# An encoder kernel in two layers: rows of maxima read back from memory, three PSUM banks passed on, later requests for the next layer's weights

## The chip, the core and the metric

The kernel runs on one core of a Trainium2 chip. The metric is the time of one execution on the device in microseconds (us). The kernel before takes 1848.21 us, the median of three runs from 1846.54 to 1849.18.

## What is computed

Two layers (DEPTH = 2) of an encoder over 256 tokens of width 2048, all in f32. Each layer normalises x, projects it, runs three mixers side by side, adds their joint projection to x, and adds a mixture of experts. Cut to what matters here:

```python
for l in range(DEPTH):
    xn = rms_norm(x, norm_mix[l])
    c_q, c_kv, k_rope, dq, dk, dv, mu, mv, mo, mg = jnp.split(xn @ w_in[l], split_at, axis=-1)
    y_mla = mla_mixer(...)          # 8 heads, dense attention
    y_dil = dilated_mixer(...)      # 12 heads, dilated attention with a bias
    y_ml = mlstm_mixer(...)         # 4 heads, forward and backward
    x = x + jnp.concatenate([y_mla, y_dil, y_ml], axis=-1) @ w_out[l]
    x = x + hier_moe(rms_norm(x, norm_ffn[l]), ...)   # 16 experts, 2 of them per token

# in mlstm_scan, for each head and direction, with m the running maximum of a token
a = jnp.exp(logw - m[..., None]) * jnp.einsum('bhtd,bhsd->bhts', qc, kc)
```

The weight matrix `a` of a head needs the negated maximum of every query token in every partition (key token): a row of 256 numbers per direction, spread over 128 partitions. These rows are what the change is about.

## The kernel before, in words

There is one instruction stream per engine, written out by hand in order and tied by semaphores: TensorE (PE) multiplies, VectorE (DVE) and ScalarE (ACT) copy results out of PSUM and do the arithmetic between, SyncE (SP) asks for the weights, GpSimd (POOL) asks for a few other transfers.

**Order of a layer on TensorE.** (1) The projections c0, c1, c2 (L1012 to L1033), then mu0, lat, mu1, up, mu2 (L1038 to L1065) and the gate rows. (2) Seven pairs of projection blocks, `product(name, u)` for u = 0 to 6 with seven products p1, p6, c11, w, p5, c21, c12 each, and one single block m14. The steps of the two attentions run between these products. (3) `queries_keys(0)`, `row_of_maxima(0)` and `(1)` (L1135 to L1137), then the output projection A, `product_a(name, u)` for u = 0 to 3. The rest of the mLSTM mixer runs between its products: scores, values, `queries_keys(1)`, `row_of_maxima(2)` and `(3)` (L1140 to L1162). (4) The output projection B. (5) The router and the experts in eight pairs i = 0 to 7, with blocks g0, u0, g1, u1 and the down projections dy0 to dy3. (6) At the end of the layer a branch over code for overfull experts (L1344 to L1385, not taken here) and the last scatter, sc0 to sc7 (L1387 to L1390), which adds the last pair's result to x.

**Rows of maxima.** `gate_rows` on VectorE (L1694 to L1712) leaves the negated maxima in `neg_m`, four partitions (the heads) by two directions by 256 tokens. `row_of_maxima(h)` (L911 to L917) spreads head h to all 128 partitions with two matmuls of a selecting column, into PSUM bank `w{h}`. From there VectorE adds gates and mask on the diagonal blocks (`masked`, L1787 to L1795), and ScalarE takes exponentials (`decays`, L2366 to L2374). VectorE multiplies with the scores (`weighted`, L1797), and TensorE reads the result in `values` (L935).

**PSUM banks.** Eight banks are given out by a table made ahead of time, `plan_banks` (L200 to L283) and `plan_queries_keys` (L316 to L324). `freed(name)` waits until the previous user of the name's bank has been copied out; `copied(name)` waits for the name itself. Before the change `bias`, mu0, mu2 and the first product p1 of stage 2 all use bank 0. The queries and keys mqa, mqb, mqc use banks 2, 3 and 4, and w0 to w3 use banks 6, 7, 5 and 5. The last dilated output do5 stands in bank 3, and `queries_keys` waits for all three of its banks before its first matmul (L891).

**Weights.** SyncE works through one list of requests in order. Each waits until its slot of a ring of six (with three spare places outside the ring) has been read for the last time (`load`, L671 to L675). In the next layer the list goes c0, c1, c2, `up`, mu0, mu1, mu2, mw, m0 and so on (L681 to L700).

**GpSimd's requests.** Per layer: in the second layer x is stored (L785) and the bias table is read again (L790). Then, in both layers, it waits for the last product of stage 2 (`c12_6`, L791) and reads x back (L794), because X holds sums during stage 2. VectorE waits for x before it adds the first product of A (L1962).

Of the kernel before, what the change touches and what calls it, by code (L numbers as in the profile page):

```python
# [20 lines left out]
F32 = mybir.dt.float32  # L21
# [5 lines left out]
P = 128  # L27
# [172 lines left out]
def plan_banks():  # L200

    b = Uses(8)
    b.once("bias", 0)
# [11 lines left out]
    b.once("mu2", 0)  # L215
# [15 lines left out]
    for u in range(N_APAIR):  # L231
        for name in PRODUCTS:
# [4 lines left out]
            if at in MLSTM_AT:  # L237
# [9 lines left out]
                if h == 2:  # L247
                    b.once("w3", 5)
# [67 lines left out]
def plan_queries_keys(b, g):  # L316

    for n, c in enumerate("abc"):
        b.once(f"mq{c}{g}", 2 + n)
    if g == 0:  # L320
        b.once("w0", 6)
        b.once("w1", 7)
    else:
        b.once("w2", 5)  # L324
# [76 lines left out]
def build(nc, a, consts, onehot, lncount, out):  # L401
    with ExitStack() as ctx:
# [42 lines left out]
        x_dram = nc.dram_tensor("x_dram", (P, KT, S), F32).ap()  # L445
        bias_dram = nc.dram_tensor("bias_dram", (H_D, 2 * S), F32).ap()
# [40 lines left out]
        vf = v_mla[:, :, :].rearrange("p t n -> p (t n)")  # L487
        hs = scr[:, 0:8 * CAP].rearrange("p (k n) -> p k n", k=4)
# [68 lines left out]
        for name, n in (("sq", 4), ("sq_sum", 1), ("xg_even", KT // 2), ("xg_odd", KT // 2), ("rstd_x", 1), ("xn_n", 1), ("a_sums", 1), ("w_sums", 3 * N_PAIR), ("lat_std", 1), ("lat_n", 1),  # L557
# [3 lines left out]
                        ("masked", H_M), ("r_ready", H_M), ("m_std", 1), ("o_gate", 1), ("y_ml", 1), ("w_rg", 1), ("sq2", N_OUT), ("acc2", N_OUT),  # L561
# [104 lines left out]
        def _(sp):  # L666
# [14 lines left out]
            for l in range(DEPTH):  # L681
# [10 lines left out]

                load("up", l, a["w_up"][l], width=3 * W_D + 1024)
# [70 lines left out]
        def _(pool):  # L764
# [16 lines left out]
            for l in range(DEPTH):  # L781
                if l:
# [7 lines left out]
                    pool.dma_start(BIAS[:, :, :], bass.AP(bias_dram.tensor, 0, [[1, P], [2 * S, H_D], [1, S + P]])).then_inc(bias_out, 16)  # L790
                pool.wait_ge(*ready(f"c12_{N_PAIR - 1}", l))  # L791
                if l:
                    pool.wait_ge(x_out, 16 * l)
                pool.dma_start(X[:, :, :], x_dram if l else a["x_t"]).then_inc(x_back, 16)  # L794
            pool.wait_ge(x_back, 16 * DEPTH)
# [3 lines left out]
        def _(pe):  # L799
# [86 lines left out]
            def queries_keys(g, l):  # L886
# [4 lines left out]
                for i in "abc":  # L891
                    pe.wait_ge(*freed(f"mq{i}{g}", l))
# [3 lines left out]
                for n in range(2):  # L896
# [4 lines left out]
                    last_b = mm(o[2], w_qk[low, n, b, H_TOP:HD_M], uc[low, b, :], False, True)  # L901
                    mm(o[1][top, :], w_qk[:, n, a, P:HD_M], uc[:, a, :], True, False)
# [7 lines left out]

            def row_of_maxima(h, l):  # L911

                name = f"w{h}"
                pe.wait_ge(*freed(name, l))
                for d in range(2):
                    last = mm(bank(name)[:, d * S:(d + 1) * S], K[0:H_M, h:h + 1].to_broadcast([H_M, P]), grow(d, 0))
                last.then_inc(*made(name))  # L917
# [94 lines left out]
            for l in range(DEPTH):  # L1012
# [123 lines left out]
                for h in range(2):  # L1136
                    row_of_maxima(h, l)  # L1137
# [1398 lines left out]
```

## Time and profile before

| | |
|---|---|
| Median of 3 runs | 1848.21 us (1846.54 to 1849.18) |
| The profiled execution, its own time | 1849.53 us |
| Its span, first to last instruction | 1847.6 us |
| TensorE busy | 1825.8 us, 99% of the span |
| VectorE, ScalarE, GpSimd busy | 738.0, 313.4, 8.5 us |
| Moved by DMA | 544.78 MB, mean 295 GB/s |
| Mean granted TensorE clock | 0.997 of full speed |

The profiled execution is one execution of its own: its time is 1.3 us above the median of the runs. Times inside a profile count from the start of the span. A busy TensorE is not one at its peak, since matmuls are pipelined and their ends are modelled. Each f32 matmul stands in the trace as two records of MATMUL and two of LDWEIGHTS.

### The profile page before, as it was taken

To read this page: it belongs to the slowest core of one execution; us is meant where nothing else is said; L and a number is where in the kernel's file an instruction comes from. 1 tells how busy PE (TensorE), PEld (TensorE's weight loads), DVE (VectorE), ACT (ScalarE), POOL (GpSimd) and SP (SyncE) were. 2 spreads that over 40 slices of the span, in tenths; PEclk is the share of its full clock that TensorE was granted. 3 is DMA by queue.
4 is the path that set the end of the run, shared out by engine and by line. 5 is a ranking of instruction groups with operands and counts; after the bars stand their busy time and mean duration, and the time that the engine had idled before them with its cause. 6 is when DMAs were issued, how large, how long until landed. Compare 5 with 4: busy or idle time off the path is not lost.

```text
span 1847.6 us, 28284 instructions
## 1 busy us (share of the span) xinstructions
PE 1825.8 (99%) x12270; PEld 1384.1 (75%) x12270; DVE 738.0 (40%) x1531; ACT 313.4 (17%) x846; POOL 8.5 (0%) x17
## 2 busy tenths in 40 slices
PE   9999999999999999999899999999999999999998
PEld 8788887899765667666597888878996666666655
DVE  3467665576202122021235675655661022121123
ACT  3123122211201111011021131231121111111010
POOL 1000000000000000000000000000000000000000
PEclk9999999999999999999999999999999999999999
DMA  9433343437999999999964342352479999999995
GB/s 384 157 139 140 134 166 156 158 146 276 361 423 422 427 427 428 426 427 427 408 238 155 125 183 103 154 204 110 193 274 368 423 424 428 427 427 427 427 427 245
DMA packets 46702, 544.78 MB, mean 295 GB/s; under 512 B 5240, under 2 KB 5368, under 8 KB 12912
## 3 DMA queue, kind: packets, MB, share of 16 engines
q1 hardware_dynamic: 44784, 531.47, 70.1%
q0 software_dynamic: 1792, 11.46, 1.6%
q8 instruction: 101, 1.65, 0.4%
q14 instruction: 25, 0.20, 0.0%
HBM read 538.68 MB, written 4.22 MB: 294 GB/s over the span
## 4 chain that ended last, share of the span: by engine, by line
PE 96%; DVE 2%; DMA 1%; issue 1%; ACT 0%; SPq 0%; DVEq 0%
PE ps L801 93%; PE ps L855 1%; DMA ring<-in_w_main 1%; PE ps L1270 1%; PE ps L871 0%; PE ps L1169 0%; DMA ring<-in_w_lat 0%; PE ps L863 0%; DVE ring L1660 0%; PE ps L1324 0%; DVE ss_a L1686 0%; DVE ss_a L1685 0%; DVE XN L1950 0%; DVE ring L1900 0%; DVE ring L1845 0%
## 5 line engine op out<-in xcount | busy, mean ns | idle before, releaser
L801 PE MATMUL ps<-ring,scr 128*64 128x256 f32 (+2 forms) x3488 | 626.6, 424 | 4.1 <-issue 4.1
L801 PEld LDWEIGHTS ps<-ring,scr 128*64 128x64 f32 (+1 forms) x3488 | 337.5, 138 | 216.0 <-issue 123.9
L801 PE MATMUL ps<-ring,XN 128*128 128x256 f32 (+2 forms) x1184 | 242.4, 361 | 2.9 <-DMA ring<-in_w_lat 1.7
L801 PEld LDWEIGHTS ps<-ring,XN 128*128 128x128 f32 x1184 | 210.7, 190 | 23.9 <-issue 4.5
L801 PE MATMUL ps<-ring,X 128*128 128x256 f32 x896 | 200.6, 379 | 0.0
L801 PE MATMUL ps<-XN,ring 128*128 128x128 f32 (+1 forms) x1312 | 196.0, 306 | 1.9 <-DVE X L1933 0.9
L801 PEld LDWEIGHTS ps<-XN,ring 128*128 128x128 f32 x1312 | 180.2, 191 | 15.0 <-issue 4.1
L801 PEld LDWEIGHTS ps<-ring,X 128*128 128x128 f32 x896 | 169.6, 190 | 22.7
L801 PE MATMUL ps<-PR,scr 128*64 128x256 f32 (+2 forms) x704 | 173.8, 402 | 0.0
L2119 DVE TENSOR_TENSOR v_mla<-scr,ps 128x256 f32<-128x256 f32 x32 | 13.5, 422 | 390.5 <-PE ps L801 390.5
L801 PE MATMUL ps<-BIAS,scr 128*64 128x256 f32 (+1 forms) x608 | 157.2, 414 | 0.0
L801 PE MATMUL ps<-XN,scr 128*64 128x256 f32 (+1 forms) x480 | 143.1, 455 | 0.0
L801 PE MATMUL ps<-PR,prob 128*128 128x256 f32 x512 | 119.1, 386 | 4.8 <-issue 4.8
L801 PE MATMUL ps<-v_mla,PR 128*128 128x128 f32 x1024 | 119.2, 276 | 1.0 <-DVE v_mla L2075 1.0
L801 PEld LDWEIGHTS ps<-v_mla,PR 128*128 128x128 f32 x1024 | 116.2, 192 | 5.1 <-issue 5.1
L801 PEld LDWEIGHTS ps<-PR,scr 128*64 128x64 f32 (+1 forms) x704 | 98.0, 144 | 25.6 <-issue 3.4
L801 PEld LDWEIGHTS ps<-PR,prob 128*128 128x128 f32 x512 | 95.9, 192 | 24.0 <-issue 11.9
L2143 DVE COPY prob<-ps 128x512 f32<-128x512 f32 x32 | 22.1, 692 | 207.4 <-PE ps L801 207.4
L801 PEld LDWEIGHTS ps<-BIAS,scr 128*64 128x64 f32 x608 | 81.8, 137 | 29.6 <-issue 2.9
L2446 ACT ACTIVATE scr<-ps,par 128x128 f32<-128x128 f32 x240 | 64.7, 407 | 219.2 <-PE ps L801 219.2
L2083 DVE TENSOR_TENSOR X<-X,ps 128x512 f32<-128x512 f32 x128 | 88.0, 688 | 31.5 <-PE ps L801 30.6
L801 PEld LDWEIGHTS ps<-XN,scr 128*64 128x64 f32 x480 | 65.8, 138 | 34.2 <-issue 25.0
(276 smaller groups left out, 1457.7 us busy)
## 6 DMA issues: line engine op xcount, KB each, us to landing
ring<-in_moe_w_gate SPq DMA_DIRECT2D x42, 2048.0 KB, 20.3
ring<-in_moe_w_down SPq DMA_DIRECT2D x38, 2048.0 KB, 23.0
ring<-in_w_main SPq DMA_DIRECT2D x36, 2048.0 KB, 9.3
ring<-in_moe_w_up SPq DMA_DIRECT2D x36, 2048.0 KB, 19.3
ring<-in_w_out_a SPq DMA_DIRECT2D x16, 1280.0 KB, 5.9
PR<-in_moe_w_up SPq DMA_DIRECT2D x10, 2048.0 KB, 16.1
XN<-in_moe_w_down SPq DMA_DIRECT2D x10, 2048.0 KB, 19.6
BIAS<-in_moe_w_up SPq DMA_DIRECT2D x10, 2048.0 KB, 18.7
```

Source lines behind the costliest of these rows:

```text
L801: return pe.matmul(o, lhsT, rhs, start=start, stop=stop, skip_group_check=True)
L855: last = pe.transpose(bank(name)[:, (kt * NT + t) * P:(kt * NT + t + 1) * P], prob[:, u % 2, j, t, kt * P:(kt + 1) * P], ident)
L1270: last = pe.transpose(bank(name)[:, q * 2 * CAP:(q + 1) * 2 * CAP], gated[:, (2 * half + q) * P:(2 * half + q + 1) * P], ident)
L2083: dve.tensor_tensor(x, x, bank(name), ALU.add).then_inc(*read(name))
L2119: dve.tensor_tensor(gated[:, half * CH:(half + 1) * CH], sgs[:, half * CH:(half + 1) * CH], bank(f"u{half}_{i}")[0:2 * CAP, 0:CH], ALU.mul ...
L2143: dve.tensor_copy(Y[:, n * 512:(n + 1) * 512], bank(f"dy{n}_{i}")[0:2 * CAP, :]).then_inc(*read(f"dy{n}_{i}"))
L2446: ins = act.activation(XG[:, 4 * n + k, :], bank(name)[:, k * 2 * CAP:(k + 1) * 2 * CAP], ACT.Copy, scale=pcol(l, R_FFN + 4 * n + k))
```

## The change

Four parts. Rows of maxima: GpSimd stores `neg_m` to memory once per layer (4 KB), and reads each head's two rows back with a partition step of zero, so that they land in all 128 partitions (256 KB per head). They land in the place of `v_mla`, two heads at a time. `row_of_maxima` goes, and `masked` and `decays` read SBUF. Heads 0 and 1 are asked for after the last output of the first attention (`ao3`), heads 2 and 3 after x has been asked for and the place's last user is done (`decayed`, a signal that takes the part of the freed bank). Banks: `bias` goes to bank 1, mu2 to bank 2. For the queries and keys mqc and mqb swap places in the first group, and the bank of mqc is waited for only after four matmuls. Requests: in the second layer SyncE waits for the previous layer's sc0 of the last scatter before it asks for `up` and all that follows it in its list.

```diff
--- before.py
+++ after.py
@@ -200,7 +200,7 @@
 def plan_banks():
 
     b = Uses(8)
-    b.once("bias", 0)
+    b.once("bias", 1)
     b.part = "layer"
     for j in range(3):
         b.once(f"c{j}", 4 + j)
@@ -212,7 +212,7 @@
     for t in range(NT):
         for j in range(4):
             b.once(f"up{t}{j}", [4, 5, 6, 7, 2, 3, 4, 5][4 * t + j])
-    b.once("mu2", 0)
+    b.once("mu2", 2)
     for d in range(2):
         b.once(f"rows{d}", 6 + d)
     for u in range(N_PAIR):
@@ -244,8 +244,6 @@
                         b.once(f"ms{h + j2}", ((5, 4), (2, 3))[h // 2][j2])
                 if h == 1:
                     plan_queries_keys(b, 1)
-                if h == 2:
-                    b.once("w3", 5)
             if at == MIX_AT:
                 for y in range(5, KT // 2):
                     b.once(f"y{y}", y - 3)
@@ -315,13 +313,8 @@
 
 def plan_queries_keys(b, g):
 
-    for n, c in enumerate("abc"):
-        b.once(f"mq{c}{g}", 2 + n)
-    if g == 0:
-        b.once("w0", 6)
-        b.once("w1", 7)
-    else:
-        b.once("w2", 5)
+    for c, n in zip("abc", (2, 4, 3) if g == 0 else (2, 3, 4)):
+        b.once(f"mq{c}{g}", n)
 
 
 
@@ -443,6 +436,8 @@
         sweep_load, sweep_pe, sweep_act, sweep_dve, sweep_own = map(
             sem, ("sweep_load", "sweep_pe", "sweep_act", "sweep_dve", "sweep_own"))
         x_dram = nc.dram_tensor("x_dram", (P, KT, S), F32).ap()
+        maxima_dram = nc.dram_tensor("maxima_dram", (H_M, 2 * S), F32).ap()
+        maxima_out, maxima_in = sem("maxima_out"), [sem(f"maxima_in{b}") for b in range(2)]
         bias_dram = nc.dram_tensor("bias_dram", (H_D, 2 * S), F32).ap()
 
         ident, flip = K[:, K_ID:K_ID + P], K[:, K_FLIP:K_FLIP + P]
@@ -485,6 +480,7 @@
         combT = scr[0:NE, 1536:1536 + S]
 
         vf = v_mla[:, :, :].rearrange("p t n -> p (t n)")
+        maxima = vf[:, 0:4 * S].rearrange("p (b d s) -> p b d s", b=2, d=2)
         hs = scr[:, 0:8 * CAP].rearrange("p (k n) -> p k n", k=4)
         sgs = scr[0:2 * CAP, 512:512 + F_E]
         XG = scr[:, 1024:1024 + KT * 2 * CAP].rearrange("p (k n) -> p k n", k=KT)
@@ -558,7 +554,7 @@
                         ("a_roped", 1), ("a_sq", 1), ("a_ss", 1), ("a_std", 1), ("a_n", 1),
                         ("d_sq", 2), ("d_ss", 2), ("u_conv", 1), ("v_ones", 1), ("rb", 1), ("d_std", 1), ("d_n", 1), ("nmax", H_A), ("d_exp", H_D), ("p_scaled", H_A + H_D),
                         ("gate_b", 1), ("gate_ln", 2), ("rows_ready", 2), ("em_ready", 1), ("uc_ready", 1),
-                        ("masked", H_M), ("r_ready", H_M), ("m_std", 1), ("o_gate", 1), ("y_ml", 1), ("w_rg", 1), ("sq2", N_OUT), ("acc2", N_OUT),
+                        ("masked", H_M), ("decayed", H_M), ("r_ready", H_M), ("m_std", 1), ("o_gate", 1), ("y_ml", 1), ("w_rg", 1), ("sq2", N_OUT), ("acc2", N_OUT),
                         ("ya_sums", 2), ("a1", N_APAIR), ("a2", N_APAIR), ("a3", N_APAIR), ("a4", N_APAIR),
                         ("y_sums", 2), ("t1", N_BPAIR), ("t2", N_BPAIR), ("t4", N_BPAIR),
                         ("e_in", 2), ("e_exp", 2), ("picked", 1), ("flags", 1), ("gm", NE), ("gw", NE // 2),
@@ -690,6 +686,8 @@
                 for j in (1, 2):
                     load(f"c{j}", l, a["w_lat12"][l, j - 1], width=KT * LAT[j][1])
 
+                if l:
+                    sp.wait_ge(*ready(f"sc0_{NE // 2 - 1}", l - 1))
                 load("up", l, a["w_up"][l], width=3 * W_D + 1024)
                 for j in range(W_M // CH):
                     load(f"mu{j}", l, a["w_main"][l, 3 * W_D // CH + j])
@@ -788,10 +786,27 @@
                     pool.wait_ge(*ready(LAST_READER[last], l - 1))
                     pool.wait_ge(*ready("mu0", l))
                     pool.dma_start(BIAS[:, :, :], bass.AP(bias_dram.tensor, 0, [[1, P], [2 * S, H_D], [1, S + P]])).then_inc(bias_out, 16)
+                def load_maxima(h):
+
+                    pool.dma_start(maxima[:, h % 2, :, :].rearrange("p d s -> p (d s)"),
+                                   bass.AP(maxima_dram.tensor, h * 2 * S, [[0, P], [1, 2 * S]])).then_inc(maxima_in[h % 2], 16)
+
+                pool.wait_ge(*after("rows_ready", l, 1))
+                if l:
+                    pool.wait_ge(maxima_in[0], 16 * H_M // 2 * l)
+                    pool.wait_ge(maxima_in[1], 16 * H_M // 2 * l)
+                pool.dma_start(maxima_dram, neg_m[:, :, :].rearrange("h d s -> h (d s)")).then_inc(maxima_out, 16)
+                pool.wait_ge(maxima_out, 16 * (l + 1))
+                pool.wait_ge(*ready(f"ao{H_A // 2 - 1}", l))
+                load_maxima(0)
+                load_maxima(1)
                 pool.wait_ge(*ready(f"c12_{N_PAIR - 1}", l))
                 if l:
                     pool.wait_ge(x_out, 16 * l)
                 pool.dma_start(X[:, :, :], x_dram if l else a["x_t"]).then_inc(x_back, 16)
+                for h in range(2, H_M):
+                    pool.wait_ge(*after("decayed", l, h - 2))
+                    load_maxima(h)
             pool.wait_ge(x_back, 16 * DEPTH)
             pool.wait_ge(bias_out, 32 + 16 * (DEPTH - 1))
 
@@ -888,7 +903,7 @@
                 a, b, c = 3 * g, 3 * g + 1, 3 * g + 2
                 top, low = slice(0, H_TOP), slice(H_TOP, P)
                 out = [[bank(f"mq{i}{g}")[:, n * S:(n + 1) * S] for i in "acb"] for n in range(2)]
-                for i in "abc":
+                for i in "ab":
                     pe.wait_ge(*freed(f"mq{i}{g}", l))
                 if g == 0:
                     pe.wait_ge(*after("uc_ready", l))
@@ -899,6 +914,8 @@
                     mm(o[2], w_qk[:, n, c, H_TOP:HD_M], uc[:, c, :], True, False)
                     last_a = mm(o[0], w_qk[top, n, b, 0:P], uc[top, b, :], False, True)
                     last_b = mm(o[2], w_qk[low, n, b, H_TOP:HD_M], uc[low, b, :], False, True)
+                    if n == 0:
+                        pe.wait_ge(*freed(f"mqc{g}", l))
                     mm(o[1][top, :], w_qk[:, n, a, P:HD_M], uc[:, a, :], True, False)
                     mm(o[1][low, :], w_qk[:, n, c, 0:H_TOP], uc[:, c, :], True, False)
                     if n == 1:
@@ -907,14 +924,6 @@
                     mm(o[1][top, :], w_qk[top, n, b, P:HD_M], uc[top, b, :], False, True)
                     last = mm(o[1][low, :], w_qk[low, n, b, 0:H_TOP], uc[low, b, :], False, True)
                 last.then_inc(*made(f"mqc{g}"))
-
-            def row_of_maxima(h, l):
-
-                name = f"w{h}"
-                pe.wait_ge(*freed(name, l))
-                for d in range(2):
-                    last = mm(bank(name)[:, d * S:(d + 1) * S], K[0:H_M, h:h + 1].to_broadcast([H_M, P]), grow(d, 0))
-                last.then_inc(*made(name))
 
             def scores(g, l):
 
@@ -1133,8 +1142,6 @@
                         step(NT * j + t - 1)
 
                 queries_keys(0, l)
-                for h in range(2):
-                    row_of_maxima(h, l)
                 pe.wait_ge(*copied(f"ao{H_A // 2 - 1}", l))
                 pe.wait_ge(*copied(f"do{H_D // 2 - 1}", l))
                 for u in range(N_APAIR):
@@ -1156,8 +1163,6 @@
                                 scores(h // 2, l)
                             if h == 1:
                                 queries_keys(1, l)
-                            if h in (1, 2):
-                                row_of_maxima(h + 1, l)
                         if at == MIX_AT:
                             mixed(l)
                 for q in range(5, KT // 2):
@@ -1787,16 +1792,16 @@
                 def masked(h):
                     if h == 0:
                         dve.wait_ge(*copied("gcols", l))
-                    dve.wait_ge(*ready(f"w{h}", l))
+                    dve.wait_ge(maxima_in[h % 2], 16 * (H_M // 2 * l + h // 2 + 1))
                     for d in range(2):
                         for at, t, b in DIAGONAL[d]:
-                            ins = dve.scalar_tensor_tensor(decay[:, h % 2, d, at:at + P], bank(f"w{h}")[:, d * S + t * P:d * S + (t + 1) * P],
+                            ins = dve.scalar_tensor_tensor(decay[:, h % 2, d, at:at + P], maxima[:, h % 2, d, t * P:(t + 1) * P],
                                                            gcol[:, 0, d, b, h:h + 1], masks[d], ALU.add, ALU.add)
                     ins.then_inc(*signal("masked"))
 
                 def weighted(h):
                     dve.wait_ge(*ready(f"ms{h}", l))
-                    dve.wait_ge(*copied(f"w{h}", l))
+                    dve.wait_ge(*after("decayed", l, h))
                     for d, lo, hi, src in ((0, 0, S, 0), (0, S, S + P, S + P), (1, 0, P, 0), (1, P, P + S, S)):
                         w = decay[:, h % 2, d, lo:hi]
                         ins = dve.tensor_tensor(w, w, bank(f"ms{h}")[:, src:src + hi - lo], ALU.mult)
@@ -2367,11 +2372,11 @@
                     act.wait_ge(*after("masked", l, h))
                     for d in range(2):
                         at, t, b = ACROSS[d]
-                        act.activation(decay[:, h % 2, d, at:at + P], bank(f"w{h}")[:, d * S + t * P:d * S + (t + 1) * P], ACT.Exp,
+                        act.activation(decay[:, h % 2, d, at:at + P], maxima[:, h % 2, d, t * P:(t + 1) * P], ACT.Exp,
                                        bias=gcol[:, 0, d, b, h:h + 1])
                         ends = decay[:, h % 2, d, :].rearrange("p (b n) -> p b n", n=P)[:, ::2, :]
                         ins = act.activation(ends, ends, ACT.Exp)
-                    ins.then_inc(*read(f"w{h}"))
+                    ins.then_inc(*signal("decayed"))
 
                 def one_way(g):
                     act.wait_ge(*after("r_ready", l, g))
```

## Rows read from the trace of the kernel before

**Rows 1.** Page, part 1: busy us (share of the span) and instructions of TensorE

```profile
PE 1825.8 (99%) x12270; PEld 1384.1 (75%) x12270; DVE 738.0 (40%) x1531; ACT 313.4 (17%) x846; POOL 8.5 (0%) x17
```

**Rows 2.** Waits of TensorE: total us, times, longest us

```profile
PE ps L801 <- issue: 10.0, 7, 3.8
...
PE ps L801 <- ACT PR L2287: 1.3, 2, 0.7
...
PE ps L801 <- DVE prob L1472: 0.9, 1, 0.9
```

**Rows 3.** Timeline, first layer, stage 3: start us, us, engine, line, records [idle before]

```profile
320.64 5.75 PE L801 MATMUL ps<-ring 128*128 128x256 f32 x32 [0.53 <-issue]
326.33 1.99 PE L801 MATMUL ps<-neg_m,K 4*128 4x256 f32 x8
328.25 2.50 PE L801 MATMUL ps<-PR,ring 128*128 128x128 f32 x20
...
354.94 1.12 PE L801 MATMUL ps<-neg_m,K 4*128 4x256 f32 x4
355.99 2.50 PE L801 MATMUL ps<-PR,ring 128*128 128x128 f32 x20
```

**Rows 4.** Tile neg_m: records on TensorE, ns min/median/max, first and last start

```profile
L801 PE MATMUL ps<-neg_m,K x32: 374/374/478, 326.3 to 1289.7; 4*128 4x256 f32 x32
```

**Rows 5.** Timeline of VectorE and TensorE, second layer, the same place

```profile
1246.42 2.15 DVE L1793 SCALAR_TENSOR_TENSOR scr<-ps,gcol,K 128x128 f32<-128x128 f32 x8
1249.54 0.69 DVE L1930 TENSOR_TENSOR X<-X,ps 128x512 f32<-128x512 f32 x1 [0.97 <-PE ps L801]
1250.14 0.42 DVE L1933 TENSOR_TENSOR X<-X,ps 128x256 f32<-128x256 f32 x1
...
1251.50 2.40 PE L801 MATMUL ps<-PR,ring 128*128 128x128 f32 x20
```

**Rows 6.** Request of x on GpSimd, landing times, and head 2's first use on VectorE

```profile
300.73 0.55 POOL L794 DMA_DIRECT2D X<-in_x_t  x1 [252.52 <-PE ps L801]
...
X<-in_x_t POOLq DMA_DIRECT2D x1, 2048.0 KB, 12.4
...
356.10 1.13 DVE L1793 SCALAR_TENSOR_TENSOR scr<-ps,gcol,K 128x128 f32<-128x128 f32 x4 [1.33 <-PE ps L801]
```

**Rows 7.** Windows: busy of PE, PEld, DVE, ACT, POOL (records); clock, DMA share, GB/s

```profile
450.00:460.00 10.00, 9.81 (x93) 8.58 (x92) 5.35 (x11) 3.39 (x7) 0.00 (x0) 1.00 0.44 156
...
860.00:870.00 10.00, 10.00 (x78) 5.41 (x76) 0.69 (x1) 0.60 (x1) 0.00 (x0) 1.00 1.02 433
```

**Rows 8.** Timeline of TensorE, where block g1 of expert pair 7 starts, each layer

```profile
879.29 0.40 PE L801 MATMUL ps<-ring,scr 128*64 128x256 f32 x1 [1.45 <-issue]
...
1797.94 0.46 PE L801 MATMUL ps<-ring,scr 128*64 128x256 f32 x1 [2.41 <-issue]
```

**Rows 9.** Timeline around the last scatter, each layer, and the first read of mu0

```profile
908.45 0.33 SPq L675 DMA_DIRECT2D ring<-in_w_lat  x1
...
915.80 0.33 SPq L675 DMA_DIRECT2D ring<-in_w_up  x1
...
919.53 8.83 PE L801 MATMUL ps<-PR,prob 128*128 128x256 f32 x32 [3.76 <-issue]
...
959.42 13.98 PE L801 MATMUL ps<-XN,ring 128*128 128x256 f32 x64
...
1836.65 7.14 PE L801 MATMUL ps<-PR,prob 128*128 128x256 f32 x32 [1.05 <-issue]
```

**Rows 10.** Windows of 2 us at the two last scatters, columns as in rows 7

```profile
922.00:924.00 2.00, 2.00 (x6) 1.55 (x6) 1.34 (x3) 0.51 (x1) 0.00 (x0) 0.50 1.14 475
...
1834.00:1836.00 2.00, 1.61 (x8) 0.29 (x4) 0.34 (x1) 0.00 (x0) 0.00 (x0) 1.00 0.00 0
```

**Rows 11.** DMA: last w_lat request to landing; the instruction queue from 916.8 to 918

```profile
ring<-in_w_lat SPq DMA_DIRECT2D x1, 1472.0 KB, 12.6
...
q8 instruction: 1, 0.02, 5.6%
```

## The prediction

> **What bounds the kernel.** I read the page first: TensorE is busy for 1825.8 us of 1847.6, and no other engine is near that [rows 1]. So a microsecond taken from TensorE's stream counts in full, unless a transfer then sets the pace. I read the waits of TensorE next, which sum to little: 10.0 us without a releaser, the longest 3.8, then 1.3 and 0.9 us for two copies out of PSUM [rows 2]. Third came the timelines of the places that the change touches, and last the DMA share in windows, because the experts' weights come at close to the engines' full rate: a share of 0.44 shortly before the experts, but 1.02 near their end [rows 7].
>
> **Rows of maxima: what goes.** Each layer loses eight matmuls, 32 records in both layers [rows 4]. What counts is the distance from their first start to the next product's start, not the records' own 374 ns, since they overlap. For heads 0 and 1 that is 328.25 - 326.33 = 1.92 us, and for one later head 355.99 - 354.94 = 1.05 us [rows 3]; the other later head repeats the latter. Per layer 1.92 + 2 x 1.05 = 4.02 us, twice: **8.0 us**. All of it is on TensorE's own chain. The switch from narrow tiles to full ones stays, as the work in front of the rows has narrow tiles too.
>
> **Rows of maxima: what comes.** Per layer one store of 4 KB and four reads of 256 KB, on GpSimd's queue. In the first layer x is asked for at 300.73 and lands 12.4 us later; head 2 is first used on VectorE at 356.10 [rows 6]. Heads 0 and 1 are asked for even before x. Head 2 is asked for when head 0's exponentials are done, which is shortly after VectorE's `masked` work, whose counterpart in the second layer ends at 1246.42 + 2.15 [rows 5], so about 25 us before its use. No read of 256 KB had to be priced before; x, of 2 MB, took 12.4 us on this queue, so I take 0 and keep 12.4 us as the upper bound of one read, which still fits. If the cover went, `masked(2)` would wait on VectorE, with the evictions of A behind it and TensorE behind these. The DMA time of 1 MB per layer falls where the engines have room. That VectorE and ScalarE read SBUF in place of PSUM is off the chain.
>
> **What is late next.** `masked(0)` and `(1)` no longer wait for TensorE, but VectorE works in order, and TensorE now reaches A sooner. In the second layer `masked` ends at 1248.57, then VectorE needs 0.69 + 0.42 us for the first product p1, whose bank c11 takes over. c11 started at 1251.50 [rows 5] and wants to start 1.92 + 0.53 earlier, at 1249.05; p1's copy is ready at about 1249.6. So 0.5 us comes back, and I take **0.4 us lost**. In the first layer I reckon none.
>
> **Banks.** With `bias` in bank 1, mu0 needn't wait: 0.9 us once. With mu2 in bank 2, the first product needn't wait for mu2's copy: 1.3 us over both layers [rows 2]. With mqc late, `queries_keys(0)` starts before do5 is copied, and the four matmuls ahead of the wait cover the rest: 0.53 us [rows 3], twice. Sum **3.3 us**. The bounds are zero and this sum; I take the whole, since each is a gap in front of an idle engine with its inputs there.
>
> **Later requests.** In the first layer the last scatter starts after 3.76 us of idle time, in the second after 1.05, with the same code in front (a branch that isn't taken into the expert loop). Its records then take 8.83 us against 7.14 [rows 9], because the granted clock is 0.50, the 1.2 GHz level, right after the idle stretch [rows 10]. So the first layer pays 2.71 + 1.69 = 4.4 us more. What differs is the traffic: in the second layer the DMA share ahead of the scatter is 0.00 [rows 10]; in the first SyncE has asked for w_lat at 908.45 and `up` at 915.80 [rows 9]. TensorE jumps over the expert loop there, and a packet of the instruction queue is in flight between 916.8 and 918 [rows 11], before the scatter's start at 919.53.
>
> The Trainium skill (Runtime: NRT & Kernel Launch, Instruction fetch mechanics) says that a taken branch to a far target forces a fetch of the target's code by DMA before execution goes on. The two layers agree with that, and by this rule alone the whole 4.4 us would go with the traffic.
>
> But only part of the traffic is moved. The w_lat request at 908.45 takes 12.6 us to land [rows 11], to about 921, and stays where it is; the code packet starts only about 1 us after `up` is asked for. The bounds are 0 and 4.4 us; neither row is nearer, and **I take 2.0 us**. The cost of the delay itself is nothing: `up` goes out at the scatter's first result, some 2 us later, and mu0, behind it, is first read at 959.42 [rows 9].
>
> **Sum.** 8.0 + 3.3 - 0.4 + 2.0 = **12.9 us**. The profiled execution's own time, 1849.53 us, becomes 1836.6. It stands 1.3 us above the median of the runs; from the median, 1848.2, I predict **1835.3 us**. A measurement of this kernel can tell about 0.2%, 3.7 us, from no change.
>
> **Rivals.** Each keeps the 10.9 us of rows and banks where nothing else is said.
>
> *The code comes at once.* The scatter of the first layer starts as in the second: 4.4 us in place of 2.0, so 1832.9. For it speaks that the second layer has no more idle time than 1.05 us. Chance 0.27.
>
> *The code stands behind w_lat.* The late requests change nothing at the branch, and the time is 1837.3. For it speaks w_lat's landing at 921, after the scatter's start. The Trainium skill (DMA: Bandwidth & Descriptors, Queues, rings and completion order) has a DMA engine drain a whole packet of one queue before it serves another; by this the code may wait for w_lat's packet, and asking for `up` later would not help. Rows 11 fit, but don't prove it. Chance 0.25.
>
> *The weights eat the gain.* TensorE waits 1.45 and 2.41 us for blocks of the last expert pair [rows 8]: the stream of weights is the bound there. If its start were not tied to TensorE, all that TensorE saves before would come back as a longer wait: nothing left of the 10.9, so 1846.2, and 1848 if the longer idle time costs clock as well. Against it: the share of 0.44 at 450 to 460 us [rows 7] shows the stream still waiting for TensorE to release slots, after all that is removed. So it starts sooner by as much. Chance 0.06.
>
> *Rows come late: slower.* Heads 2 and 3 stand behind x on GpSimd's queue. If a read took longer than the 25 us that it has, by L us, each layer would lose about L; both layers together lose the 12.9 us gained from L = 6.5 us on, and it is a measurable loss from L = 8.3, that is a read of over 33 us. With 40 us: 1835.3 + 2 x 15 = 1865. Against it: x took 12.4 us with eight times the bytes. Chance 0.02.
>
> *The change doesn't do what it says*: rows still on TensorE, or banks that wait for another user. The bank table gives each of the moved names a bank that is long free, so 0.02, at about 1845.
>
> **Numbers.** The forecast has 0.38 and is the likeliest; the rivals have 0.27, 0.25, 0.06, 0.02 and 0.02. The low end is the code at once, no loss on VectorE and no half clock in the second layer's g1 either (1.7 us, priced like the scatter's): 1848.2 - 11.3 - 4.4 - 1.7 = 1830.8, so 1831.0. The high end is the code behind w_lat with one more stretch of half clock, 1837.3 + 1.7 = 1839.0, and half a microsecond of scatter: 1839.5. Faster by over 0.2% (under 1844.5): the first three, 0.90, and 0.03 from the others, 0.93. Within 0.2%: the weights' case, 0.05. Slower: 0.02.
>
> **What the new profile would show.** No records on neg_m from TensorE, and A's first product right behind `queries_keys`. No wait for L2287 or L1472, and no 0.53 us ahead of `queries_keys(0)`. In the second layer a short wait for VectorE at c11 of pair 0. The idle time ahead of the first layer's last scatter between 1.05 and 3.76 us, and whether the clock falls behind it, decides between the first three cases. The waits in front of g1 of pair 7 stay near 1.45 and 2.41; if they grow by several microseconds, the weights eat the gain. I am wrong if VectorE waits for a maxima transfer with TensorE behind it, or if a new gap opens where a bank changed its user.

## The result, and the profile after

The changed kernel took **1840.41 us** (median of 7 runs; the one at 1889.13 is disturbed and left out of the comparison, as is one of late_from_c2 below at 6933.86), the kernel before 1848.21. The ratio is 0.9947, 95% interval [0.9937, 0.9957]: 9.8 us less, between 7.9 and 11.6. The forecast was 1835.3, so 12.9 us less, with a range from 1831.0 to 1839.5. By the ratio the time is 1838.4, inside it; the median of the seven runs is 0.9 us above its high end, that of the six undisturbed ones, 1839.7, is 0.2 us above. A second set of runs of the same kernel (below) gave 1840.63 and 0.9946.

Page of the changed kernel: span, then part 1.

```profile
span 1837.3 us, 28234 instructions
PE 1818.3 (99%) x12238; PEld 1381.0 (75%) x12238; DVE 736.8 (40%) x1531; ACT 314.3 (17%) x846; POOL 13.9 (1%) x27
```

TensorE has lost 32 records and 7.5 us of busy time against [rows 1]: the rows of maxima. It remains the engine that bounds the kernel. The waits of TensorE, as in [rows 2]:

```profile
PE ps L816 <- issue: 9.5, 6, 4.9
PE ps L816 <- DMA ring<-in_w_lat: 2.0, 1, 2.0
PE ps L816 <- DVE eps L1452: 1.1, 1, 1.1
```

The two waits for copies, 1.3 and 0.9 us, are gone. But the longest wait has grown from 3.8 to 4.9 us. The timeline around stage 3 in the second layer, which answers to [rows 3, 5]:

```profile
1234.52 5.78 PE L816 MATMUL ps<-ring 128*128 128x256 f32 x32
...
1240.23 2.50 PE L816 MATMUL ps<-PR,ring 128*128 128x128 f32 x20
...
1240.95 2.18 DVE L1798 SCALAR_TENSOR_TENSOR scr<-v_mla,gcol,K 128x128 f32<-128x128 f32 x8
...
1243.05 0.68 DVE L1935 TENSOR_TENSOR X<-X,ps 128x512 f32<-128x512 f32 x1
1243.65 0.41 DVE L1938 TENSOR_TENSOR X<-X,ps 128x256 f32<-128x256 f32 x1
...
1244.80 1.39 PE L816 MATMUL ps<-PR,ring 128*128 128x128 f32 x11
```

`queries_keys(0)` has no 0.53 us in front of it, the first product follows it at once, and c11 of pair 0 starts without a wait. Last, the places where TensorE is idle, as in [rows 8, 9]; the third row is the last scatter of the first layer:

```profile
7.33 22.29 PE L816 MATMUL ps<-ring,XN 128*128 128x192 f32 x128 [1.98 <-DMA ring<-in_w_lat]
...
874.92 0.40 PE L816 MATMUL ps<-ring,scr 128*64 128x256 f32 x1 [1.89 <-issue]
...
916.31 8.75 PE L816 MATMUL ps<-PR,prob 128*128 128x256 f32 x32 [4.90 <-issue]
...
1789.42 0.40 PE L816 MATMUL ps<-ring,scr 128*64 128x256 f32 x1 [1.70 <-issue]
```

The stall that the late requests were to shorten is longer than before, 4.90 us against 3.76, and its records still take 8.75 us. SyncE's requests, the windows in the stall (columns as in [rows 7]), and the DMA queues between 911 and 916.3 us (packets, MB, share of the 16 engines):

```profile
892.97 11.44 SPq L671 DMA_DIRECT2D ring<-in_w_lat  x2
918.39 0.33 SPq L671 DMA_DIRECT2D ring<-in_w_up  x1
```

```profile
908.00:910.00 2.00, 2.00 (x12) 0.77 (x10) 0.00 (x0) 0.60 (x1) 0.00 (x0) 1.00 0.92 389
910.00:912.00 2.00, 1.41 (x8) 0.27 (x4) 0.55 (x1) 0.00 (x0) 0.00 (x0) 1.00 0.55 226
...
914.00:916.00 2.00, 0.00 (x0) 0.00 (x0) 0.00 (x0) 0.00 (x0) 0.00 (x0) 1.00 0.07 22
```

```profile
q1 hardware_dynamic: 53, 0.52, 23.8%
q8 instruction: 2, 0.03, 4.0%
```

So `up` did go out late, at 918.39. The only weights in the engines at the jump were those of w_lat, and TensorE stood idle all the same. The stall can be taken apart with the packets of the instruction queue, which carry TensorE's code. In the kernel before, the last product ends at 915.77, the code packet starts 1.09 us later, takes 1.07, and the scatter starts 1.60 after it: 3.76 us. In the changed kernel the product ends at 911.41, the packet starts 1.04 us later, takes 2.20, and 1.66 us follow: 4.90 (another code packet, at 911.94, is done before it). The growth is the time of the packet itself. In the second layer of the changed kernel the packet starts at 1823.87, 1.96 us *before* the product's end, and 0.53 us of idle time is left.

### The profile page after: what moved, and what is told of

The parts are those of the page before. It is cut to its first block, busy times and chain, and to the rows that moved or that the text cites. A ratio compares the mean times of both kernels' runs of the same rounds, so it can differ in the third digit from the quotient of the medians.

```text
span 1837.3 us, 28234 instructions
## 1 busy us (share of the span) xinstructions
PE 1818.3 (99%) x12238; PEld 1381.0 (75%) x12238; DVE 736.8 (40%) x1531; ACT 314.3 (17%) x846; POOL 13.9 (1%) x27
## 4 chain that ended last, share of the span: by engine, by line
PE 98%; DVE 1%; issue 1%; DMA 0%; SPq 0%; DVEq 0%
PE ps L816 94%; PE ps L870 1%; PE ps L1174 1%; PE ps L1275 1%; PE ps L886 0%; DMA ring<-in_w_lat 0%; PE ps L878 0%; PE ps L1329 0%; DVE XN L1955 0%; DVE ring L1905 0%; DVE ring L1850 0%; DVE ring L1840 0%; PE ps L1082 0%; PE ps L1055 0%; DVE X L1938 0%
```

## The experiments

What was open: is the code that the jump needs held up behind `up` (theory U), behind w_lat (theory L), or does the place of the code in its 16 KB packets decide (theory P)? And are rows and banks worth what they were priced at? Each run was compared with the kernel before in its own job; its medians there were 1848.84, 1848.27 and 1848.91.

### The late requests alone, four ways

**no_late** is the changed kernel without the wait:

```
-                if l:
-                    sp.wait_ge(*ready(f"sc0_{NE // 2 - 1}", l - 1))
                 load("up", l, a["w_up"][l], width=3 * W_D + 1024)
```

> The changed kernel without the late requests: `up` and what follows are asked for as soon as their slots are free, as before. If the late requests are worth something at the branch (theory U: the code packet stands behind `up`), the idle time ahead of the first layer's last scatter grows from the 4.90 us of the changed kernel to 7 us or more, and the time by 2 to 4 us. If the packet stands behind w_lat alone (theory L), the idle time stays between 3.5 and 5 us, its records stay at 8.8 us, and the time is that of the changed kernel, about 1838 to 1839, within 1 us.

Measured: 1839.21 us, ratio 0.9952 [0.9939, 0.9965], so the same as with the wait. Timeline of TensorE in no_late at the last scatter, then the queues from 914 to 916 us:

```profile
911.50 3.26 PE L814 MATMUL ps<-PR,prob 128*128 128x256 f32 x14 [3.45 <-issue]
916.96 4.15 PE L814 MATMUL ps<-PR,prob 128*128 128x256 f32 x18 [2.21 <-issue]
```

```profile
q1 hardware_dynamic: 65, 0.85, 102.5%
q8 instruction: 1, 0.02, 3.0%
```

There are two stalls. The one at the jump is there with and without `up` in the engines: over all profiles that ask for w_lat as before it is 2.94, 3.59 and 4.90 us with the late request, and 1.87, 2.80, 3.34, 3.45 and 3.76 without it (no_branch, which has no jump, left out). A second, of 2.21 us, opens in the middle of the scatter, while a code packet is in flight among the packets of `up`. The kernel before does not have it, and with the wait it is absent again: that is what the late request buys, for a stall that the other parts of the change had opened. The medians don't show it: 0.9952 against 0.9947 is within their intervals. What they leave open, the packets answer. The next code packet starts 3.18 us after the scatter in no_late, and 3.3 to 3.7 us after it in the four other profiles with w_lat and `up` asked for as before; with the late request it starts 0.6 us after it in all three.

**late_from_c1** moves the wait up, ahead of the loop that asks for c1 and c2 of w_lat; **late_from_c2** puts it ahead of c2 only.

```
+                if l:
+                    sp.wait_ge(*ready(f"sc0_{NE // 2 - 1}", l - 1))
                 for j in (1, 2):
                     load(f"c{j}", l, a["w_lat12"][l, j - 1], width=KT * LAT[j][1])
...
-                if l:
-                    sp.wait_ge(*ready(f"sc0_{NE // 2 - 1}", l - 1))
                 load("up", l, a["w_up"][l], width=3 * W_D + 1024)
```

> The changed kernel with the wait for sc0 two requests earlier, ahead of the w_lat loads c1 and c2. Theory L (the code packet stands behind the packets of w_lat): the idle time ahead of the first layer's last scatter falls from 4.90 us to the second layer's 0.5 to 1.1, the scatter's records fall from 8.75 to 7.15 us since the clock isn't lowered, and the time falls by 3.8 + 1.6 = 5.4 us or a little less, to about 1833. TensorE doesn't wait for c1, which has some 17 us from the request to its use. Theory U: no change at the branch. Theory P (the place of the code in its pages sets the stall, not traffic): no change at the branch either.

> The changed kernel with the wait for sc0 ahead of c2 alone; c1 is asked for as before. Theory L: the engines still have c0's and c1's packets when the code is asked for, but half of w_lat's bytes are gone, so the idle time is between 1 and 3.5 us, and the time between that of the changed kernel and that of the wait ahead of c1. Theories U and P: idle time stays at 4.9 us.

Measured: 1833.96 us, ratio 0.9927 [0.9914, 0.9941], and 1833.72 us, 0.9919 [0.9904, 0.9933]. The last scatter of the first layer in late_from_c1, and in late_from_c2:

```profile
910.06 7.17 PE L816 MATMUL ps<-PR,prob 128*128 128x256 f32 x32 [0.77 <-issue]
```

```profile
911.53 7.17 PE L816 MATMUL ps<-PR,prob 128*128 128x256 f32 x32 [1.46 <-issue]
```

With c1 and c2 out of the way the stall falls from 4.90 to 0.77 us, with only c2 out to 1.46, and the records take 7.17 us, the full clock. The DMA share of late_from_c1 is 0.03 from 905 to 909 us, where the changed kernel has 1.04, and its code packet starts 1.73 us before the last product ends, as in the second layer. Theory L holds for the stall at the jump. The cost of asking later is none that shows: the requests stand at 911.19, c1 and c2 land 7.6 us later in the median of the two, at about 917.3 and 920.8, and c0's products keep TensorE at work from 917.06 to 937.

**no_branch** leaves out on TensorE the branch and the loop for experts with more tokens than their slots hold, which this data never enters, and keeps w_lat as it is.

> The changed kernel without TensorE's code for overfull experts (the branch, the two register loads and the jumped-over loop are left out on TensorE; the inputs here never take it). All theories that put the stall on the jump (L, U and P) expect no idle time to speak of ahead of both last scatters, under 0.5 us, no lowered clock behind them, and 4.9 + 1.6 + 0.5 = 7.0 us less than the changed kernel, about 1831.5. If the idle time stays, the stall is not the jump's but that of a copy out of PSUM or of another wait.

Measured: 1830.51 us, ratio 0.9901 [0.9886, 0.9915]. Both last scatters start without idle time; the first layer's:

```profile
911.25 7.17 PE L816 MATMUL ps<-PR,prob 128*128 128x256 f32 x32
```

No code packet is in flight near this place (the next one starts at 920.07). So it takes both, a jump and w_lat's requests in flight. Either alone, late_from_c1 and no_branch show, costs less than 1 us. The run doesn't separate the jump from the two register loads and the wait for the flags that belong to the same code and went with it; for the jump speaks the code packet, which ends 1.5 to 1.7 us ahead of the scatter wherever the branch is kept.

### Each part on the kernel before

**only_rows** has the rows of maxima through memory and nothing else of the change; **only_banks** the bank numbers and the late wait for mqc; **only_late** the wait ahead of `up`; **before_late_c1** the wait ahead of c1, as above, but in the kernel before.

> The kernel before with the rows of maxima through memory alone: banks and the request for up stay as before. My sum: TensorE loses 4.02 us per layer, 8.0 us in all, the reads are hidden, and nothing or 0.4 us comes back at c11 of the second layer: ratio about 0.9957 (8.0 of 1848). The gaps of the banks must all still be there (0.9 and 0.68 us for the copies, 0.53 ahead of queries_keys(0)). If the rows were worth less than their distances on TensorE, because a transfer or VectorE takes over, the saving is well under 8 us and TensorE shows a wait for VectorE or for a maxima read. A shift of the last scatter against the pages of its code can add a second gap of about 2 us inside it, as in no_late, or not.

Measured: 1844.22 us, ratio 0.9977 [0.9968, 0.9985], 4.3 us less in place of 8.0. Timeline of TensorE in only_rows, both layers from `queries_keys(0)` to a later row of stage 3, and between them the end of the first layer:

```profile
320.46 5.75 PE L814 MATMUL ps<-ring 128*128 128x256 f32 x32 [0.53 <-issue]
...
460.12 5.44 PE L814 MATMUL ps<-v_mla,PR 128*128 128x128 f32 x32 [0.50 <-DVE v_mla L2076]
...
906.61 7.09 PE L814 MATMUL ps<-ring,scr 128*64 128x512 f32 x32 [1.74 <-issue]
916.50 4.95 PE L814 MATMUL ps<-PR,prob 128*128 128x256 f32 x14 [2.80 <-issue]
922.34 4.15 PE L814 MATMUL ps<-PR,prob 128*128 128x256 f32 x18 [0.89 <-issue]
...
1237.18 5.75 PE L814 MATMUL ps<-ring 128*128 128x256 f32 x32 [0.53 <-issue]
...
1377.07 3.81 PE L814 MATMUL ps<-v_mla,PR 128*128 128x128 f32 x32 [0.50 <-DVE v_mla L2076]
```

The same distance in only_late, which has the rows on TensorE, is 467.57 - 323.88 = 143.69 us in the first layer and 1387.61 - 1243.92 = 143.69 in the second. Here it is 139.66 and 139.89: **4.03 and 3.80 us** less, 7.8 in all. The six profiles with rows and banks changed in which no half clock falls into the distance have 139.67 to 139.70 in both layers. So the saving is there, and it is lost elsewhere. At the end of the first layer the idle times sum to 1.74 + 2.80 + 0.89 = 5.43 us against 3.76 before, in the second 0.75 + 0.95 = 1.70 against 1.05: 2.3 us back. The rest is clock: over its 12 runs the granted clock averaged 0.9961, over the 35 of the kernel before 0.9971, and 0.0010 of 1848 is 1.8 us. 7.8 - 2.3 - 1.8 = 3.7, beside 4.3 measured.

> The kernel before with bias in bank 1, mu2 in bank 2 and mqc late (its bank order too), all else as before. My sum: 0.9 + 1.3 + 2 x 0.53 = 3.3 us, ratio about 0.9982, and the three kinds of gap are gone from TensorE's waits while no new one opens. Rival: each gap moves to the next user of a bank or the next transfer, and the ratio is 1.000.

Measured: 1847.06 us, ratio 0.9986 [0.9974, 0.9998], 2.6 us less. The waits for L2287, for L1472 and the 0.53 us are gone, and no new one stands in their place. The last scatter of the first layer reads

```profile
920.15 7.14 PE L801 MATMUL ps<-PR,prob 128*128 128x256 f32 x32 [3.34 <-issue]
```

The stall at the jump was 3.34 us here, 0.4 less than before, and the mean clock 0.9965, worth 1.1 us: 3.3 + 0.4 - 1.1 = 2.6.

> The kernel before with only the wait ahead of the request for up. Theory L (the jump's code stands behind w_lat): the idle time ahead of the first layer's last scatter stays between 3 and 5 us, lowered clock behind it, and the time is that of before within 1 us, ratio 0.9995 to 1.0005. Theory U (it stands behind up): idle 1.1 us, no lowered clock, 4.4 us less, ratio 0.9976. Theory P (the place of the code in its pages decides whether a second fetch falls into the scatter): before had no second gap, so the wait has nothing to take away here and the time stays.

Measured: 1850.96 us, ratio 1.0015 [1.0006, 1.0024]: **slower**. Timeline of TensorE in only_late:

```profile
914.36 7.09 PE L803 MATMUL ps<-ring,scr 128*64 128x512 f32 x32 [1.87 <-issue]
924.39 8.83 PE L803 MATMUL ps<-PR,prob 128*128 128x256 f32 x32 [2.94 <-issue]
```

The stall at the jump stays, with the clock lowered behind it. There is no second stall for the wait to remove. Of the 2.8 us lost, 4.81 - 3.76 = 1.0 is the longer idle time at this place and 1.1 the mean clock (0.9965); 0.7 us stays open, within the interval. That the wait causes these is not shown; it gains nothing.

> The kernel before with the wait for the last scatter's first result ahead of the requests for c1, c2 and what follows, so that only c0 of w_lat is in flight at the jump. Theory L: the idle time ahead of the first layer's last scatter falls from 3.76 to about 1 us, the clock stays at full rate behind it, and the time is 4.4 us shorter, ratio 0.9976. Theory P (the place of the code): 3.76 us stay, ratio 1.000. If later requests have a price of their own, it shows as a wait of TensorE for c1 or c2 in the second layer, up to 2 us.

Measured: 1845.74 us, ratio 0.9987 [0.9978, 0.9996], 2.4 us less, in place of 4.4. The mechanism is as expected, since the last scatter of the first layer reads

```profile
915.24 7.14 PE L803 MATMUL ps<-PR,prob 128*128 128x256 f32 x32 [1.02 <-issue]
```

with 3.76 - 1.02 = 2.74 us less idle time and the full clock. The 1.7 us of lowered clock that should have gone too don't show in the median: the mean clock of its 12 runs, 0.9975, is only 0.0004, 0.7 us, above that of the kernel before. 2.74 + 0.7 = 3.4 us, and the interval reaches from 0.7 to 4.1.

### The same kernels again, and the code shifted

> The kernel after, unchanged, to see what of its profile is fixed and to compare it with the next run on the same chip. If the place of its stall is fixed by the program, the idle time ahead of the first layer's last scatter is 4.9 us again; if the 4.90 was one draw of when the code packets meet the packets of w_lat, it lies anywhere from 3 to 5. The median should come at about 1840, ratio 0.9947.

Measured: 1840.63 us, ratio 0.9946 [0.993, 0.9961]. In its profile the stall ahead of the last scatter is 3.59 us, and the last product of the experts has one of its own:

```profile
906.16 7.09 PE L816 MATMUL ps<-ring,scr 128*64 128x512 f32 x32 [1.52 <-issue]
916.83 8.83 PE L816 MATMUL ps<-PR,prob 128*128 128x256 f32 x32 [3.59 <-issue]
```

So the same program shows 4.90 and 3.59 us, and the growth from 3.76 is no fixed effect of the change.

> The kernel late_from_c1 again, in one job with the kernel after. Theory L: under 1 us of idle time ahead of the first layer's last scatter again, and the time is that of the kernel after less 3 to 5 us, ratio to before about 0.9925. Rival (its time was luck with stretches of lowered clock): the medians of the two differ by under 1.5 us.

Measured: 1831.89 us, ratio 0.9903 [0.9887, 0.992], 8.7 us under the changed kernel in the same job, more than the 3 to 5 expected. The last scatter of the first layer:

```profile
910.40 7.44 PE L816 MATMUL ps<-PR,prob 128*128 128x256 f32 x32 [0.79 <-issue]
```

The spans of the two profiles differ by 1839.0 - 1829.4 = 9.6 us: 3.59 - 0.79 = 2.8 is the stall, 1.7 the clock behind it, 1.5 - 0.2 = 1.3 the wait ahead of the last product, and 3.4 are two more stretches of half clock in after_again, where this profile has none before its very end; 0.4 is left. That the edit removes those two is not shown; the stall and the clock behind it, 4.5 us, are what it accounts for. With ratios of 0.9927 and 0.9903 in two jobs this kernel beats both the kernel before and the changed one, and keeps all the code.

**no_late_shifted** is no_late with three wide warm-up products less and thirteen narrow ones more at the start:

```
-            keep_running(0, 10)
+            keep_running(0, 7)
+            for _ in range(13):
+                mm(ps[:, 0, 0:1], ones[:, :], ones[:, 0:1])
```

> The kernel no_late with 40 instructions more on TensorE at the program's start (three wide warm-up products less, thirteen of one column more), hidden in its wait for the first weights, so that all of TensorE's code lies 40 instructions later against the borders of its 16 KB packets. If the 2.21 us of idle time inside the first layer's last scatter are the code packet behind the packet border that lay after 14 of its records, that gap must go, the one ahead of the scatter (w_lat) stays at 3 to 5 us, and the time is about 2 us less than that of no_late (ratio 0.994). Rival: if the gap were a wait for PSUM or for a copy, it stays at the same record whatever the place of the code. Another border may come to lie where it costs: in the last scatter of the second layer at most 0.6 us, as its engines are idle.

Measured: 1838.10 us, ratio 0.9935 [0.992, 0.9949], against 0.9952 for no_late, in line with 2 us, though the intervals overlap. The last scatter of the first layer is whole again:

```profile
916.66 7.14 PE L814 MATMUL ps<-PR,prob 128*128 128x256 f32 x32 [1.87 <-issue]
```

The stall in its middle is gone by moving code alone. The engine's inputs were the same, and the DMA engines as full (share 1.00 from 918 to 920 us, against 1.05 from 914 to 916 in no_late). So it was a code packet. In no_late and only_rows, both without the rows and without the wait, the border lay after the same 14 records; in the kernel before there is no stall in the scatter, so the border must lie elsewhere. That is the part of theory P that holds. The stall at the jump, 1.87 us, was shorter than the 3 to 5 us that I expected.

## Why the prediction was right, and where it failed

**Rows of maxima, 8.0 us: right.** The distances give 4.03 + 3.80 = 7.8 us in only_rows, and 4.0 us in each layer with the banks changed too. The reads cost nothing: four a layer, 3.5 us each from request to landing (x, the row I bounded them with, took 12.2). Head 2's was requested at 329.24 and VectorE first used it at 352.00.

**What comes back, 0.4 us: it didn't.** I let c11 wait for p1's copy, behind `masked`. But `masked` needs no records of TensorE any more, and it began 0.72 us after p1 began (1240.95 against 1240.23). The copy of p1 was done at 1244.06, and c11 started at 1244.80. From the start of `queries_keys(0)` to c11 it is 10.28 us, where it was 12.17 with the same two products between: 1.89 us less, all of what the row of maxima had cost. The reckoning had put the end of `masked` where it was before, at 1248.57, while TensorE alone moved.

**Banks, 3.3 us: right**, by the rows in only_banks and in the changed kernel; none of the gaps moved to another user of a bank.

**Later requests, 2.0 us: wrong.** This is the step that failed. I had put the stall down to traffic in general and, between 0 and 4.4 us, taken about the middle, though the last code packet started only about 1 us after `up` was asked for. At the jump the late request took nothing off: the stall comes with w_lat's requests, all of which were out before `up` was asked for, and it goes when they are held back (0.77, 0.79 and 1.02 us). The rival "The code stands behind w_lat", with 1837.3 us and a chance of 0.25, was the right one. The sum with 0 for this term and for the loss at c11 is 8.0 + 3.3 = 11.3 us, beside 9.8 measured (7.9 to 11.6). That the time still fell into the range is no merit of the 2.0 us: the range had its high end from this rival, and it lies 3.1 us from the forecast and 1.1 us from the rival's figure. The Trainium skill (DMA: Bandwidth & Descriptors, Queues, rings and completion order) has an engine drain a whole packet of one queue before it serves another, which is what this looks like, but no run here shows the order inside one engine. Nor does the amount of traffic set the length: between 911 and 916.3 us w_lat's packets took only 23.8% of the engines in the changed kernel, and its stall is the longest of all.

**What I did not see** is the second stall. Taking eight matmuls out of each layer moves all later code against its packets' borders, so that one came to lie inside the last scatter, 14 records in, where the engines are full and the next code packet comes 3.2 to 3.7 us after the jump. The late request removes it (2.21 us in no_late, none in the changed kernel), and that is its whole worth here. Alone on the kernel before it gains nothing (1.0015). The Trainium skill (Runtime: NRT & Kernel Launch, Instruction fetch mechanics) calls the cost of such a crossing "mostly hidden". With idle engines the traces agree: a packet starts at 1826.93 in the changed kernel's last scatter, and the records take 7.14 us without a wait. With full ones two of the profiles show 0.89 and 2.21 us.

**The weights eat the gain: no.** The waits ahead of g1 of pair 7 were 1.89 and 1.70 us against 1.45 and 2.41; they did not take up what TensorE saved. The half clock that followed the 2.41 us in the kernel before is absent behind the 1.70 us, as the low end of the range had it; in no_late the wait is 2.62 us and the half clock is back. But a relative of this rival exists: the last product of the experts starts right as its block of weights lands. In the kernel before it landed at 908.60, by the trace's landing events, and the product started at 908.69; in only_rows at 906.52, product at 906.61. Four of the 13 profiles taken have such a wait, of 0.75 to 1.87 us: only_late, after_again and no_branch in one layer, only_rows in both. In four of these five cases the last of the block's sixteen landing events came 1.2 to 2.2 us after the fifteenth, so the late share of one of the 16 DMA engines would explain them; in the fifth (only_rows, second layer) it came 0.15 us after.

**Why single parts don't add up.** Parts measured alone gave -4.3, -2.6 and +2.8 us, a sum of -4.1 beside -9.8 for the whole. What the parts take off TensorE's own rows does add up (4.0 us in each layer for the rows, and none of the banks' waits left). What doesn't is the stall at the jump, which takes another length each time (1.87 to 4.90 us where all of w_lat is in flight), and the number of stretches at half clock, each 3.41 us long (once twice that) and worth 1.7 us: from none to four before the end of the span in the profiles taken.

## What to carry to other kernels

A jump on the engine that bounds the kernel was cheap here with idle DMA engines (0.5 to 1.1 us) and dear with weights in flight (1.87 to 4.90); look at what is in flight before the jump, not at what is asked for last. Move requests that nobody needs for 20 us behind the jump, and start with those that go out earliest. And when a change takes instructions out, later code falls differently into its packets: a saving read from rows can be right and yet be hidden by a stall that has merely moved, so look for idle time "by issue" inside stretches that had none.

## What the runs showed of the hardware

- **From the end of the code packet to the first record after a jump: about 1.6 us.** In the trace the packet started at 916.86 us in the kernel before, took 1.07, and TensorE resumed at 919.53; in before_late_c1 912.48 + 1.18 and 915.24; in only_late 921.74 + 1.07 and 924.39. With idle engines the packet starts 1.4 to 2.0 us before TensorE is done with its last product, so that 0.5 to 1.1 us of idle time is left. With all of w_lat in flight it starts between 0.6 us before and 1.1 us after that end.
- **Half clock after a long stall.** Behind the last scatter's stall in the first layer the granted clock fell to 0.50, the 1.2 GHz level, after 2.80, 2.94, 3.59, 3.76 and 4.90 us of idle time; after 3.34 and 3.45 it did not, nor after any of 1.87 or less. At g1 of pair 7 shorter waits had the same effect: the clock fell with 1.95, 2.07, 2.09, 2.41, 2.62 and 3.31 us (the last for twice as long), and with none of 1.94 or less. So a long stall costs its length and often 1.7 us more, but not every time.
- **Half clock without a long stall.** Other stretches have no wait of more than 0.5 us near them, as at 455.4 and 1370.1 us in the changed kernel. Thirteen stretches in 11 of the 13 profiles fall at this one place of a layer, between the router's products and the first products of the experts; why there is open. Between two single profiles of this kernel these stretches alone can make several microseconds, so the comparisons above rest on 4 to 12 runs of each kernel.
